# A hybrid decoder layer on one core: key rounds in the gate rounds' order with 512-column loads, half of the decays moved to the gate round, eight transposes one sub-block later

## The reference

```python
h = rmsnorm(x, g_mix_pre)
proj = h @ w_in                      # 2048 x 8208
mq, mk, mv, mo, mi, mf, rq, rk, rv, rg = split(proj)
mq, mk = silu(causal_dwconv([mq, mk], conv_w, conv_b))      # 4 taps
hm = mlstm_chunkwise(mq, mk, mv, mi + b_igate, mf + b_fgate)  # 8 heads of 128, chunks of 128
hm = head_rmsnorm(hm) * sigmoid(mo)
hr = retention_chunkwise(rotary(rq), rotary(rk), rv)          # 8 heads of 128
hr = head_rmsnorm(hr) * silu(rg)
x = x + rmsnorm([hm, hr] @ w_out, g_mix_post)
h = rmsnorm(x, g_ffn_pre)
x = x + rmsnorm((silu(h @ w_gate) * (h @ w_up)) @ w_down, g_ffn_post)
```

## Time and profile before

| | |
|---|---|
| median of 3 runs | 1232.44 us (1231.84 to 1232.49) |
| the profiled execution | 1232.54 us |
| its span | 1230.8 us |
| TensorE matmul busy | 1218.8 us, 99% |
| VectorE busy | 715.5 us, 58% |
| ScalarE busy | 600.4 us, 49% |
| moved | 229.49 MB, 186 GB/s over the span |

### The profile page before, as it was taken

How to read it: one execution, slowest core, us unless ns; L and a number is a source line. 1 busy time by engine, 2 the same in 40 slices (tenths; PEclk the granted TensorE clock), 3 DMA queues, 4 the chain that set the end, 5 groups by cost and what they waited for, 6 DMA issues and landing times.

```text
span 1230.8 us, 15775 instructions
## 1 busy us (share of the span) xinstructions
PE 1218.8 (99%) x5899; PEld 1024.3 (83%) x5899; DVE 715.5 (58%) x919; ACT 600.4 (49%) x789; POOL 14.1 (1%) x35
## 2 busy tenths in 40 slices
PE   8999999999999999999999999999999999999997
PEld 7888888888888888888888888888888888888886
DVE  6657878877686646654555454454455454444444
ACT  5654765574655645744444444444444444343442
POOL 2000200000000000000000000000000000000000
PEclk9999999999999999999999999999999999999999
DMA  8656858668685556456565656556565665555551
GB/s 314 210 149 152 210 141 191 162 130 231 153 190 177 206 198 229 134 184 205 173 199 180 198 175 200 185 190 197 178 191 184 204 209 202 192 185 204 191 185 69
DMA packets 120553, 229.49 MB, mean 186 GB/s; under 512 B 6080, under 2 KB 22720, under 8 KB 120000
## 3 DMA queue, kind: packets, MB, share of 16 engines
q1 hardware_dynamic: 120224, 226.84, 60.7%
q0 software_dynamic: 288, 2.10, 0.4%
HBM read 226.83 MB, written 2.10 MB: 186 GB/s over the span
## 4 chain that ended last, share of the span: by engine, by line
PE 95%; DVE 2%; DMA 2%; ACT 0%; issue 0%; SPq 0%; DVEq 0%; ACTq 0%
PE bank L1288 93%; DMA raw<-in_w_in 1%; PE bank L1586 1%; DMA resid<-in_x 1%; DVE w_lo L818 1%; DVE gT L1045 0%; PE bank L1293 0%; PE bank L1502 0%; DVE h L845 0%; ACT w_hi L481 0%; DVE resid L1160 0%; PE bank L1559 0%; DVE pre L1008 0%; DVE hT L831 0%; DVE pre L1048 0%
## 5 line engine op out<-in xcount | busy, mean ns | idle before, releaser
L818 DVE TENSOR_TENSOR w_lo<-raw,w_hi 128x1024 fp32r<-128x1024 f32 x420 | 513.5, 1225 | 480.2 <-ACT w_hi L481 479.4
L481 ACT ACTIVATE w_hi<-raw 128x1024 fp32r<-128x1024 f32 x420 | 444.1, 1060 | 567.8 <-PE bank L1288 550.9
L1288 PE MATMUL bank<-w_hi,h2T 128*128 128x512 f32 x1376 | 426.6, 390 | 0.0
L1288 PEld LDWEIGHTS bank<-w_hi,h2T 128*128 128x128 f32 x1376 | 258.3, 188 | 53.2
L1288 PE MATMUL bank<-hT,w_hi 128*128 128x512 f32 x768 | 271.6, 397 | 0.0
L1288 PE MATMUL bank<-w_lo,h2T 128*128 128x512 f32 x688 | 267.7, 389 | 0.0
L1288 PE MATMUL bank<-w_hi,ffT 128*128 128x512 f32 x704 | 217.3, 389 | 0.0
L1288 PE MATMUL bank<-hT,w_lo 128*128 128x256 f32 x768 | 214.6, 279 | 0.0
L1288 PEld LDWEIGHTS bank<-hT,w_hi 128*128 128x128 f32 x768 | 144.0, 187 | 32.3
L1288 PEld LDWEIGHTS bank<-w_hi,ffT 128*128 128x128 f32 x704 | 132.2, 188 | 27.5
L1288 PEld LDWEIGHTS bank<-w_lo,h2T 128*128 128x128 f32 x688 | 129.2, 188 | 26.5
(11 more groups left out here) (173 smaller groups left out, 563.5 us busy)
## 6 DMA issues: line engine op xcount, KB each, us to landing
raw<-in_w_in SPq DMA_DIRECT2D x63, 1024.0 KB, 10.2
raw<-in_w_gate SPq DMA_DIRECT2D x44, 1024.0 KB, 5.2
raw<-in_w_up SPq DMA_DIRECT2D x44, 1024.0 KB, 5.2
raw<-in_w_down SPq DMA_DIRECT2D x44, 1024.0 KB, 5.0
raw<-in_w_out SPq DMA_DIRECT2D x16, 1024.0 KB, 5.0
resid<-in_x SPq DMA_DIRECT2D x2, 1024.0 KB, 7.1
out<-resid SPq DMA_DIRECT2D x8, 256.0 KB, 2.5
raw<-in_w_in SPq DMA_DIRECT2D x2, 512.0 KB, 6.6
```

The source lines that it names most:

```text
L481: act.activation(part_of(w_hi, rnd, s), src, ACT.Copy).then_inc(hi_done, 1)
L818: dve.tensor_tensor(part_of(w_lo, rnd, s), raw_sub(rnd, s)[1], part_of(w_hi, rnd, s).bitcast(F32), ALU.subtract).then_inc(lo_done, 1)
L1288: return pe.matmul(out_, lhsT, rhs, start=start, stop=stop, skip_group_check=True)
```

## The change

Three things are changed, with the waits that follow from them.

1. Key rounds get the order of the gate rounds (now `LATE_ORDER`), load 512 columns a run, and run on TensorE through `wide_columns`; unit 0 now ends with sub-block 4 and unit 1 begins with sub-block 2. Quarters are needed for sub-blocks 0, 1, 3, 4 and come free after 3, 6, 7, 8 blocks.
2. `decays_at`: in the key round of group 0 ScalarE makes the decays of heads 0 and 1 in step 2, of 2 in step 3, of 3 in step 4, and those of heads 4 to 7 in steps 0 and 1 of the gate round. `scores`, `weighted` and `turned` wait for the decays of the heads whose spread rows lie in their bank.
3. The transposes of tiles 8 to 15 follow sub-blocks 4, 6, 8 and 10 of the first value rounds instead of 3, 5, 7 and 9, and wait only for the pieces of x and for the banks that they use.

```diff
 def later_tiles(s):
-    return range(s + 5, s + 7) if s % 2 and 3 <= s < 10 else ()
+    return range(s + 4, s + 6) if s % 2 == 0 and 4 <= s <= 10 else ()
...
-GATE_ORDER = ((0, 0), (0, 1), (1, 0), (0, 2), (0, 3), (1, 1), (1, 2), (1, 3))
-WIDE_ORDERS = (QUERY_ORDER, None, GATE_ORDER)
+LATE_ORDER = ((0, 0), (0, 1), (1, 0), (0, 2), (0, 3), (1, 1), (1, 2), (1, 3))
+WIDE_ORDERS = (QUERY_ORDER, LATE_ORDER, LATE_ORDER)
...
+def decays_at(rnd, s):
+    return {(R_IN + 1, 2): (0, 1), (R_IN + 1, 3): (2,), (R_IN + 1, 4): (3,),
+            (R_IN + 2, 0): (4, 5), (R_IN + 2, 1): (6, 7)}.get((rnd, s), ())
...
-                            if n == 1:
-                                src = in_rows(8 * (q % 2), 8, col + (q // 2) * 256, 256)
-                            else:
-                                src = in_rows(4 * q, 4, col, 512)
+                            src = in_rows(4 * q, 4, col, 512)
...
                     head_step(rnd, s)
                     ahead(rnd, s)
+                    if rnd == R_IN + 2:
+                        for h in decays_at(rnd, s):
+                            mlstm_decay(h)
                     mixer_step(rnd, s)
...
-                    if rnd == R_IN + 1 and 2 <= s < 5:
-                        for h in range(3 * s - 6, min(3 * s - 3, HEADS)):
+                    if rnd == R_IN + 1:
+                        for h in decays_at(rnd, s):
                             mlstm_decay(h)
...
                 if later_tiles(k):
-                    pe.wait_ge(h_ready, CHUNKS * TT)
-                    pe.wait_ge(xT_lo, k + 1)
+                    pe.wait_ge(h_ready, CHUNKS + later_tiles(k)[0] // 4 + 1)
+                    pe.wait_ge(xT_lo, later_tiles(k)[1] - 8 + 1)
...
             def scores(group, n):
-                pe.wait_ge(decay_ready, 2 * HEADS)
+                pe.wait_ge(decay_ready, HEADS + 2)
...
             def weighted(group, n):
...
+                pe.wait_ge(decay_ready, HEADS + 4 + 2 * (n % 2))
...
             def turned(group, n):
...
+                pe.wait_ge(decay_ready, 2 * HEADS)
...
-            for u in range(2):
-                unit_columns(R_IN + 1, u, event_of(R_IN + 1, u), hT,
-                             after=lambda s: spread_rows(s) if 2 * s < HEADS else None)
+            wide_columns(R_IN + 1, event_of(R_IN + 1, 0), hT, LATE_ORDER,
+                         after=lambda s: spread_rows(s) if 2 * s < HEADS else None)
...
-                for u in range(2):
-                    unit_columns(3 * j + (gate_round(0) + 2), u,
-                                 6 * j + event_of(gate_round(0) + 2, u), hT)
+                wide_columns(3 * j + (gate_round(0) + 2), 6 * j + event_of(gate_round(0) + 2, 0), hT,
+                             LATE_ORDER)
```

More of the change, by code:

```diff
@@ L407, in _ @@
             for q in range(4):
-                load(R_OUT, q, rows(w_out, 4 * q, 4, 0, 512), free=free_after(GATE_ORDER))
+                load(R_OUT, q, rows(w_out, 4 * q, 4, 0, 512), free=free_after(LATE_ORDER))
             with sp.Fori(1, 4) as g:
@@ L1310, in sub_columns @@
                 ins.then_inc(sub_done, 1)
[L1312 to L1321, removed]
             def wide_columns(rnd, event, act_T, order, before=None, after=None):
@@ L1515, in after @@
                             turned(group, (s - 5) // 2)
-                wide_columns(rnd, event, hT, GATE_ORDER, before, after)
+                wide_columns(rnd, event, hT, LATE_ORDER, before, after)
             def left_over(group):
```

## The result

The changed kernel takes 1234.94 us, median of 14 runs (1234.59 to 1235.71); before, 1232.30 of 14 (1231.77 to 1236.99). The ratio of the runs is 1.0017, 95% interval 1.0009 to 1.0025; that of the two medians is 1.0021 (one execution of the kernel before took 4.7 us more than its median, none of the changed kernel more than 0.8). That is inside the range, and at the 0.2% that the chances went by. The forecast was 1233.6: it had the sign and most of the places, and about half of the size.

A forecast was written before the change was run, and what follows sets the result against it. TensorE was taken as the bound, busy 1218.8 of 1230.8 us, with 1.9 us of waits. 1232.54 + 0.44 + 0.61 + 0.61 - 0.51 = 1233.7, less 0.1 for the profiled execution: 1233.6 us, range 1231.6 to 1236.2.

The forecast's parts named there:

- Transposes: First four late transposes, moved behind sub-block 4, leave TensorE's idle stretch and cost +0.44 us; other groups 0.
- kT: Key rounds: TensorE waits for unit 0's kT before first scores, +0.61 us each in groups 0 and 1, 0 in 2 and 3.
- reloading its function table: Gate sub-blocks 0 and 1: ScalarE some 3 us behind with decays and table; TensorE loses 0, at most +0.5 us.
- The removed wait: Group 2: 2 KB runs speed key loads, ending TensorE's wait for probabilities, -0.51 us.
- The gate loads: Group 1: gate quarter 2, issued later, lands at 229 to 230.5, wanted at 228.4; cost 0, bounds 0 and +0.9 us.
- The microsecond of slack: Group 1: quarter 2 one microsecond late costs nothing, as the scores' wait gives 0.6 us and slack before `weighted` is 0.3.
- the scores' wait: Wait for kT, about half a microsecond, delays TensorE and adds slack before first `weighted`, so the two waits don't add up.
- rival 2: Group 1: bunched gate loads land late, ScalarE's copy of gate block 1 delays kT and scores: +5, 1238 us; chance 0.09.
- Rival 1: Key rounds: kT isn't late, VectorE packs the chain better, the order costs nothing: 1232.4 us; chance 0.12.
- 3: Wider key loads aren't faster but wanted earlier; TensorE waits in two groups, +4.4 us, 1237.3 with the transposes; chance 0.04.
- 4: Whole kernel faster by over 0.2%, needing 2.5 us where TensorE idles 1.9; chance 0.03.

The follow-up runs named there:

- exchanged rows: Changed kernel with gate-round loads of quarters 2 and 3 reading each other's rows, sizes and order kept: 1233.33 us, ratio 0.9998.
- keys not scaled: Changed kernel without VectorE's scaling of unit sums of keys in groups 0 and 1: 1234.29 us, ratio 1.0010.
- narrow runs: Changed kernel with each 512-column key load cut into two of 256 columns (1 KB runs), same rows and order: 1239.76 us, ratio 1.0048.

## Why the prediction was right in sign and short in size

**Transposes: right.** +0.44 predicted, +0.40 in the profile.

**kT: right in group 1, half right in group 0.** The chain was put at 8.6 us and is 8.59; TensorE starts 0.06 behind it where I took 0.13, so 0.53 instead of 0.61. In group 0 I named VectorE's chain alone. ScalarE's table load ends with it, and taking 0.7 us from VectorE won nothing. I had written of "reloading its function table" only for the decays.

**The removed wait: right.** -0.67 for -0.51, and -0.66 to -0.68 in every trace with the late order. But the reason that I gave, the 2 KB runs, isn't shown for it, since 1 KB runs in that order do as well there. Its size varies with the execution of the kernel before.

**The gate loads: the term that was mis-sized.** The prediction: "If they land in line, quarter 2 lands at 229 to 230.5 [...] One microsecond late costs TensorE nothing [...]; I take 0, bounds 0 and +0.9." It landed at 231.24 and cost 1.13. But the changed kernel issues its quarter 1 0.7 later than the prediction's 217.4 (218.10), so on the prediction's clock the landing is 230.5, the upper end of its own range. The microsecond of slack was right too: with the landing at 230.3 (exchanged rows) TensorE doesn't wait, and with 5.90 us from landing to product the wait of the changed kernel begins at 230.1, which is 229.4 on that clock. So the term was mis-sized in the step from these numbers to 0: 230.5 less 229.4 is 1.1 us, above the bound of 0.9, and three quarters of the range from 229 to 230.5 cost something. That the landing fitted was luck in part: the upper end is 217.4 + 9.0 + 4.1 (one fast window of the earlier trace rows), and the two loads took 6.5 and 6.7. That the scores' wait is taken off this one holds too: the start of the product hangs on the landing alone, and where the wait for kT was gone (keys not scaled) its 0.44 us were waited here. This is rival 2's mechanism at another instruction: a load that is late holds ScalarE, and what stands behind it is not kT but the right half of unit 1.

**The pace: not foreseen.** The other +0.7, in group 2, is in no wait. Products of w_hi in the query and key rounds of group 2, 256 to 304 us, after:

```profile
L1294 PE MATMUL bank<-hT,w_hi 128*128 128x512 f32 x133 | 47.3, 400 | 0.0
```

and before, 255 to 301:

```profile
L1288 PE MATMUL bank<-hT,w_hi 128*128 128x512 f32 x130 | 45.5, 393 | 0.0
```

The same products take 400 ns instead of 393. The windows of 284 to 300 us, after and then before, in the columns of the earlier trace rows, show the granted clock at 1.00 in both (the 2.4 GHz level) and three products fewer:

```profile
284.00:300.00 16.00, 16.00 (x92) 13.87 (x91) 11.45 (x13) 8.11 (x10) 0.00 (x0) 1.00 0.73 164
```

```profile
284.00:300.00 16.00, 16.00 (x95) 14.12 (x94) 11.21 (x14) 7.03 (x9) 0.00 (x0) 1.00 0.81 230
```

By start times, from the second to the sixteenth product of a sub-block it is 2.43 or 2.48 us, and a pace lasts until small products (scores, products with v, transposes of heads) come between or, in one place of the second trace of the kernel before, TensorE waits (0.55 us at 291); the stretches at the lower clock are left out of this. Of the 96 sub-blocks of the four groups, 35 run at the slower one after (39 in the second trace), 23 before (29 in the second), 34 with narrow runs, and 19 to 25 in all other experiments. What picks the pace is open: the two experiments with exchanged rows and unscaled keys give TensorE the changed kernel's very instructions and don't show the +0.7.

**Sum.** Predicted 0.44 + 0.61 + 0.61 - 0.51 = +1.15. Found in the profile: 0.40 + 0.42 + 0.53 - 0.67 for these terms (0.68), 1.13 for the load, and 0.76 of other steps (0.73 in group 2's rounds, 0.03 for all the rest): 2.57. Rival 1 falls, as kT is late; of 2 the late load is there, but in front of other work and for 1.1 us instead of 5; 3 falls, as the waits that it foresaw in front of wide key loads are not there; 4 falls with the sign.

## What to carry to other kernels

Where an engine works in order, look at what stands behind each instruction that waits for a load: moving the urgent work in front of it took away two waits of TensorE, 1.7 us, though no load came earlier. When an order is changed so that a buffer is freed later, work out the late end of the next load's landing, with those in line ahead of it and by the slowest of its kind in the trace, and carry that end through to the sum: here it stood in the prediction and was priced at 0. Take waits of 0.5 us behind loads from more than one execution before counting on their removal.

## What the runs showed of the hardware

Loads of equal size and shape don't take equal times: 1 MB in 2 KB runs took 6.7 us and the next 4.1 (6.6 to 7.2 and 3.4 to 4.1 in eight traces), and with the rows that they read exchanged each took 5.4 (one trace). The rate also varies between executions: one load of the kernel before landed at 282.5 in one and at 288.6 in another. TensorE has two paces for the same products at the same granted clock, 2% apart (2.43 and 2.48 us for a sub-block's fourteen steps), and keeps one for up to twelve sub-blocks, some 33 us. Behind a wait of 2.69 us in the kernel with narrow loads its granted clock was at 0.50 for 3.4 us, from 1.1 us after the wait's end, and that cost 1.5 us; behind waits of 2.0 us in two other traces (the transposes alone, the second of the kernel before) it stayed at 1.00. A load of ScalarE's function table takes 1.28 us, and where it stood between a weight copy and kT, TensorE lost 0.43.
